# Second layer's expert outputs: summed in PSUM by products with gated selection matrices instead of a round trip through DRAM

## The reference, cut to what matters

```
def moe_ffn(h, ...):                       # per layer; h is the normed, modulated input
    aff = sigmoid(h @ router_w)            # (tokens, 16)
    ... two experts of the best group per token; w = aff of the two / their sum
    gates = one_hot-weighted w             # (tokens, 16)
    for e in range(16):
        he = silu(h @ w_gate[e]) * (h @ w_up[e])      # 1024 -> 512
        y = y + gates[..., e:e + 1] * (he @ w_down[e])  # 512 -> 1024
    return y
# after it: x = x + gate_ffn * y           (gate_ffn: one value per feature, from the conditioning)
# at the end: rms_norm(x, final_norm_g)
```

## Time and profile before

| | us |
|---|---|
| three runs | 3882.34, 1355.3, 1358.66 (median 1358.66) |
| profiled execution, its own time | 1355.8 |
| span of its profile, first to last instruction | 1354.0 |
| PE / weight loads / DVE / ACT / POOL busy | 1126.1 / 529.5 / 428.9 / 297.5 / 64.4 |
| mean granted TensorE clock | 0.921 of 2.4 GHz |
| moved by DMA | 344.03 MB, mean 254 GB/s |

### The profile page before, as it was taken

One profiled execution on the slowest core, in us unless ns is written; L12 is line 12 of the kernel. 1 busy time (PEld: TensorE's weight loads), 2 busy tenths in 40 slices (PEclk: granted clock), 3 DMA queues, 4 the chain that ended last, 5 costly groups with the idle time before them and its releaser, 6 DMA issues.

```text
span 1354.0 us, 15872 instructions
## 1 busy us (share of the span) xinstructions
PE 1126.1 (83%) x6028; PEld 529.5 (39%) x6028; DVE 428.9 (32%) x1021; ACT 297.5 (22%) x694; POOL 64.4 (5%) x71
## 2 busy tenths in 40 slices
PE   4899979978997799999983699988898699994454
PEld 2364433444543333333331446533367233332223
DVE  4111344668714401111110521346673311110003
ACT  2220112426603211111110512013262111110002
POOL 2000011100000200000001000011000100000001
PEclk9899989989999799999986799989899899996676
DMA  9713102939993699999999211306715699999972
GB/s 338 268 63 117 70 0 77 419 126 354 343 378 124 249 337 363 394 396 395 404 392 392 101 62 63 123 2 275 283 36 211 230 374 386 401 415 415 403 289 94
DMA packets 86997, 344.03 MB, mean 254 GB/s; under 512 B 6918, under 2 KB 42187, under 8 KB 64395
## 3 DMA queue, kind: packets, MB, share of 16 engines
q1 hardware_dynamic: 67728, 309.68, 59.2%
q10 hardware_dynamic: 15195, 19.86, 4.3%
q0 software_dynamic: 4000, 13.49, 2.8%
HBM read 300.92 MB, written 42.07 MB: 253 GB/s over the span
## 4 chain that ended last, share of the span: by engine, by line
PE 66%; DMA 18%; DVE 8%; ACT 4%; issue 2%; SPq 1%; POOL 1%; ACTq 1%; POOLq 0%; DVEq 0%
PE ps L946 14%; PE ps L541 12%; DMA ring<-in_exp_w_up 10%; PE ps L969 7%; PE ps L836 6%; PE ps L550 6%; PE ps L484 4%; PE ps L506 3%; DMA slots<-arena 2%; DMA ring<-in_w_mod 2%; PE ps L713 2%; PE ps L729 2%; PE ps L800 1%; PE ps L778 1%; DMA arena<-slots,slot_ids 1%
## 5 line engine op out<-in xcount | busy, mean ns | idle before, releaser
L946 PE MATMUL ps<-ring,arena 128*32 128x256 f32 (+1 forms) x1344 | 197.0, 529 | 47.2 <-DMA ring<-in_exp_w_up 47.2
L541 PE MATMUL ps<-u,ring 128*128 128x512 f32 (+1 forms) x416 | 167.0, 562 | 9.5 <-ACT u L1771 4.0
L484 PE MATMUL ps<-cst,arena 128*128 128x128 f32 (+1 forms) x534 | 99.5, 306 | 64.4 <-DVE arena L1471 33.0
L946 PEld LDWEIGHTS ps<-ring,arena 128*32 128x32 f32 (+1 forms) x1344 | 70.8, 135 | 156.1 <-issue 147.2
L1627 DVE TENSOR_TENSOR arena<-arena,ps 128x128 f32<-128x128 f32 (+1 forms) x59 | 27.2, 503 | 327.0 <-ACT arena L1954 327.0
L484 PEld LDWEIGHTS ps<-cst,arena 128*128 128x128 f32 (+1 forms) x534 | 62.3, 151 | 150.6 <-issue 79.5
L541 PEld LDWEIGHTS ps<-u,ring 128*128 128x128 f32 x416 | 79.8, 193 | 94.2 <-issue 89.3
L969 PE MATMUL ps<-arena 128*32 128x256 f32 (+1 forms) x672 | 94.4, 485 | 1.6 <-ACT arena L1963 1.6
L946 PE MATMUL ps<-arena 128*64 128x512 f32 (+1 forms) x544 | 81.7, 523 | 15.9 <-DMA arena<-in_exp_w_up 15.9
L1954 ACT ACTIVATE arena<-ps 128x256 f32<-128x256 f32 (+1 forms) x44 | 15.3, 348 | 328.1 <-PE ps L946 307.4
L836 PE MATMUL ps<-u,ring 128*128 128x512 f32 (+1 forms) x256 | 83.6, 487 | 1.3 <-DVE h L1452 1.3
(11 more groups left out here) (294 smaller groups left out, 1095.3 us busy)
## 6 DMA issues: line engine op xcount, KB each, us to landing
ring<-in_w_mod SPq DMA_DIRECT2D x24, 2048.0 KB, 10.0
ring<-in_exp_w_gate SPq DMA_DIRECT2D x22, 2048.0 KB, 17.8
ring<-in_exp_w_up SPq DMA_DIRECT2D x22, 2048.0 KB, 21.5
arena<-in_exp_w_down SPq DMA_DIRECT2D x22, 2048.0 KB, 18.2
slots<-zeros SPq DMA_DIRECT2D x4, 6144.0 KB, 42.2
arena<-in_exp_w_gate SPq DMA_DIRECT2D x10, 2048.0 KB, 18.7
u<-in_exp_w_down SPq DMA_DIRECT2D x10, 2048.0 KB, 19.3
arena<-in_exp_w_up SPq DMA_DIRECT2D x10, 2048.0 KB, 24.1
```

The costliest lines, as they stand in the source:

```text
L484: return nc.tensor.transpose(dst, src, ident[0:n, 0:n])
L541: last = nc.tensor.matmul(bank[row:row + width, 0:T - c0], w[:, k, n:n + width], u[:, k, c0:T], start=(k == 0), stop=(k == KT - 1))
L946: last = nc.tensor.matmul(ps[n * part:n * part + n, 2 + b % 2, 0:2 * width].rearrange("p (s n) -> p s n", s=2), x_k, pair[:, :, a:a + widt ...
```

## The change

In the second layer the expert outputs no longer go to DRAM. For each block a selection matrix `sel` (block slots on partitions, 256 tokens on the free axis) is built, which holds the token's gate where the token's slot is this one and zero elsewhere. A product of `sel` with the block's output adds it, in token rows, to four PSUM banks (3, 7 for tile 2; 4, 5 for tile 3) that hold the sum over all blocks.

- `seed_sums`: 8 float32 products for each token tile with the identity put the residual `h` into these banks as the first term.
- `spread_ffn_gates`: 16 products put the feature gates in rows, in the two layouts of a block; ACT copies them. `take_y` then multiplies by them instead of copying.
- `router` on DVE builds diagonal matrices of slots and gates (8 instructions); `spread_rows` on PE makes rows of them on all partitions (2 products); ACT keeps them (`keep_rows`).
- `select` on DVE: two instructions for each block. `combine` on PE: 4 products for a block of 64, 8 for one of 32.
- With four banks taken, blocks no longer alternate between two banks for gate_up and down results.
- The last norm works on token rows: ACT squares with a running sum, DVE scales by root and by the final gain, which two broadcast DMAs bring.
- Gone in the second layer: all `store_y`, the waits for them, the four gathers, `add_experts`, `split_norm("final")` and the transposes back.

```
 def experts(l):   # PE, before the blocks
+    if l == 1: pe.wait_ge(S("ffn_kept"), 2)
...
+def seed_sums(t):
+    for half in range(2):
+        for m in range(4):
+            nc.tensor.matmul(ps[:, sum_bank(t, half), P * m:P * m + P], h[:, 4 * half + m, P * t:P * t + P],
+                             ident, start=(m == 0), stop=False, skip_group_check=True)
+def spread_ffn_gates():
+    pe.wait_ge(S("ut_taken"), ut_count(1, TT - 1, 1) + 1)
+    for n, bank in ((64, 2), (32, 6)):
+        for part in range(P // n):
+            for m in range(n // 16):
+                k = n // 16 * part + m
+                last = nc.tensor.matmul(ps[n * part:n * part + n, bank, P * m:P * m + P],
+                                        mod[:, 1, V_GATE_FFN + k, 1:2].to_broadcast([P, n]), ident,
+                                        start=True, stop=True, tile_position=(0, n * part))
+    last.then_inc(S("ffn_spread"), 1)
...
+def spread_rows():
+    pe.wait_ge(S("diag_ready"), 1)
+    ...
+    nc.tensor.matmul(ps[:, 6, :], ones[:, :], diag[:, 0:2, :], start=True, stop=True)
+    nc.tensor.matmul(ps[:, 0, :], ones[:, :], diag[:, 2:4, :], start=True, stop=True).then_inc(S("rows_spread"), 1)
+def combine(b):
+    n = blocks[b][3]
+    pe.wait_ge(S("sel_ready"), ...); pe.wait_ge(S("y_ready", l), p * nb + (b + 3))
+    order_of = [(2, 0), (3, 1), (3, 0), (2, 1)] if n == 64 else (
+        [(2, 0), (2, 2), (3, 1), (3, 3), (2, 1), (2, 3), (3, 0), (3, 2)])
+    pe.wait_ge(S("combined"), p * (2 * nb) + (2 * b + 4))
+    for i, (t, part) in enumerate(order_of):
+        if 2 * i == len(order_of):
+            last.then_inc(S("combined"), 1)
+            if n == 32: pe.wait_ge(S("combined"), p * (2 * nb) + (2 * b + 5))
+        rows = slice(n * part, n * part + n)
+        width = 8 * n
+        half, at_col = divmod(width * part, 512)
+        last = nc.tensor.matmul(ps[:, sum_bank(t, half), at_col:at_col + width],
+                                sel[rows, b % 2, P * (t - 2):P * (t - 2) + P], y_sb[rows, b % 2, 0:width],
+                                start=False, stop=True, skip_group_check=True)
+    last.then_inc(S("combined"), 1)
...
     gate_up(0)
+    if l == 1: spread_rows()
     turn_hidden(0)
     for b in range(nb - 1):
         gate_up(b + 1)
         if b + 2 < nb:
             turn_x(b + 2)
         project_down(b)
+        if l == 1 and b: combine(b - 1)
         turn_hidden(b + 1)
     project_down(nb - 1)
+    if l == 1:
+        combine(nb - 2)
+        combine(nb - 1)
...
     # PE, order around the experts of a layer
     route(l, range(4, KT))
+    if l == 1: seed_sums(2)
     router(l)
     to_rows(l)
+    if l == 1:
+        seed_sums(3)
+        spread_ffn_gates()
     places(l)
     experts(l)
-    add_experts(l)
-    ... the transposes of the output
+    if l == 0: add_experts(l)
...
     # DVE
     def take_y(b):
         dve.wait_ge(S("down_done", l), p * nb + (nb + b + 1))
-        dve.wait_ge(S(f"y_stored{b % 2}", l), ...)
-        v.tensor_copy(y_sb[:, b % 2, 0:n], ps[:, 6 + b % 2, 0:n]).then_inc(S("y_ready", l), 1)
+        # l == 1:
+        dve.wait_ge(S("combined"), p * (2 * nb) + (2 * b + 2))
+        tt(y_sb[:, b % 2, 0:n], ps[:, down_bank(l, b), 0:n], ffn_rows[blocks[b][3]], ALU.mult) ...
+    def select(b):
+        ...
+        stt(sel_two, slot_rows, slot_at[:, b:b + 1], gate_rows, ALU.is_equal, ALU.mult) ...
+        tt(sel[:, b % 2, :], sel_two[:, 0, :], sel_two[:, 1, :], ALU.add) ...
     hidden(0)
     for b in range(nb - 1):
+        if l == 1: select(b)
         hidden(b + 1)
         take_y(b)
+    if l == 1: select(nb - 1)
     take_y(nb - 1)
...
+    for i, t in enumerate((2, 3)):   # the end on DVE, after two small additions
+        dve.wait_ge(S("root_ready"), i + 1)
         for half in range(2):
-            emptied(v.tensor_copy(tok[...], claim(f"out{t}{half}")))
+            stt(tok[:, t, 512 * half:512 * half + 512], ps[:, sum_bank(t, half), :], small[:, 32 + i:33 + i],
+                final_rows[half], ALU.mult, ALU.mult).then_inc(S("out_ready"), 1)
...
     # ACT, before the blocks of the second layer
+    for half in range(2):
+        act.dma_start(final_rows[half], final_norm_g[...].partition_broadcast(P)) ...
+    act.wait_ge(S("ffn_spread"), 1)
+    nc.scalar.copy(ffn_rows[64], ps[:, 2, :]).then_inc(S("ffn_kept"), 1)
+    nc.scalar.copy(ffn_rows[32], ps[:, 6, 0:256]).then_inc(S("ffn_kept"), 1)
...
-            store_y(b)
+            if l == 0: store_y(b)
...
+    # ACT, after the blocks of the second layer
+    exp_and_ln()
+    act.wait_ge(S("combined"), n_more * (2 * nb) + (2 * nb + 4))
+    for i, t in enumerate((2, 3)):
+        for half in range(2):
+            last = a(x_blk[:, 2 * i + half, :], ps[:, sum_bank(t, half), :], ACT.Square, accum_out=small[...])
+        last.then_inc(S("sums_squared"), 1)
+    for i in range(2):
+        act.wait_ge(S("squares_added"), i + 1)
+        rsqrt(small[:, 32 + i:33 + i], small[:, 32 + i:33 + i], S("root_ready"), 1.0 / DM, small[:, 20:21])
```

More of the change, by code:

```diff
@@ L104, in shape_constants @@
     c[:, C_TOK:C_TOK + TT] = P * np.arange(TT)[None, :] + i[:, None]
+    blocks = expert_blocks(1)
+    assert len(blocks) <= C_CAP - C_SLOT
+    for b, (_, r, a, n) in enumerate(blocks):
+        c[:, C_SLOT + b] = first_row(r) + a + i % n
+        c[:, C_CAP + b] = capacity(1, r)
     return c
@@ L978, in experts @@
                     gate_up(0)
+                    if l == 1:
+                        spread_rows()
                     turn_hidden(0)
@@ L1058, in _ @@
                 route(l, range(4, KT))
+                if l == 1:
+                    seed_sums(2)
                 router(l)
                 to_rows(l)
+                if l == 1:
+                    seed_sums(3)
+                    spread_ffn_gates()
                 places(l)
                 experts(l)
-                add_experts(l)
[L1064 to L1071, removed]
+                if l == 0:
+                    add_experts(l)
         @block.vector
@@ L1696, in _ @@
                 experts(l)
-                add_experts(l, "1mix" if l == 0 else "final")
-            for t in (2, 3):
+                if l == 0:
+                    add_experts(l, "1mix")
+            for i, t in enumerate((2, 3)):
+                dve.wait_ge(S("sums_squared"), i + 2)
+                tt(small[:, 32 + i:33 + i], small[:, 24 + 2 * i:25 + 2 * i], small[:, 25 + 2 * i:26 + 2 * i],
+                   ALU.add).then_inc(S("squares_added"), 1)
+            dve.wait_ge(S("const_landed"), 16 * (3 + n_vec_dmas))
+            for i, t in enumerate((2, 3)):
+                dve.wait_ge(S("root_ready"), i + 1)
                 for half in range(2):
-                    emptied(v.tensor_copy(tok[:, t, 512 * half:512 * half + 512], claim(f"out{t}{half}")))
+                    stt(tok[:, t, 512 * half:512 * half + 512], ps[:, sum_bank(t, half), :], small[:, 32 + i:33 + i],
+                        final_rows[half], ALU.mult, ALU.mult).then_inc(S("out_ready"), 1)
         @block.scalar
@@ L1976, in experts @@
                     silu(0)
+                    if l == 1:
+                        keep_rows()
                     copy_hidden(0)
@@ L2033, in _ @@
                 experts(l)
-            split_norm("final", "y1")
         @block.gpsimd
```

145 lines of the change are left out of this document (121 added, 24 removed).

## The result

The changed kernel took 1338.12 us (median of 4 runs, 1335.06 to 1339.24) against 1356.98 for the kernel before, a ratio of 0.9854 with a 95% interval of 0.9837 to 0.9871: 1.5% faster, which is less than 2% but clear of 1. (The ratio is estimated from the single executions and need not be the quotient of the two medians.) Forecast were 1337 us. The profiled span is 1335.6 us, to the tenth what the sum gave, and that is partly luck: the front cost 1.7 us less than forecast, and an offset of 1.8 us that was in no term cancelled it.

What follows compares the result with a forecast made beforehand. PE was taken to bound the stretch of large blocks and the weight DMAs that of small ones. 1354.0 + 0.9 + 4.7 - 24 = 1335.6 us of span, plus 1.8 around it, gave 1337; range 1323 to 1352.

Steps and rivals of the forecast that it cites:

- Step 1: From the last gate_up to the end of the span, 47.1 us before: 23.7 us saved, taken as 24.
- Step 2: Large blocks: combines on PE release o8's down weights 9.2 us later, queues run dry, last weights land 0.9 us later.
- Step 3: Ahead of the blocks: seeds and gate spread on PE delay the counting product and everything after by 4.7 us.
- DMA alone: Block stretch: queues hold work through the large blocks, the stores' 11.2 us come off in full, 1325.3 us; chance 0.17.
- Products in series: Combines: products of one combine don't overlap, +16.2 us by the last weights, 1360.3 us in all; chance 0.10.
- A second pass: Hidden round trip kept by the change, as a second pass or a wait for x rows; chance about 0.02.
- Steps at nothing: Around the blocks: spread_rows, keep_rows, select, diagonals and single gate_up and down banks cost nothing; spread_rows uncovered would cost 1.93 us.

Runs made afterwards that it cites:

- mixed order: The changed kernel with the second layer's experts reordered so that large and small blocks alternate: 1329.7 us, ratio 0.9793 to the kernel before.
- the one in series: The changed kernel with the four products of each 64-slot combine run one after another, a wait between the two pairs: 1352.0 us, ratio 0.997 to the kernel before.

## Why the prediction was right, step by step

- **Step 1, the end: right.** 23.7 to 24 us were forecast and 24.2 measured (22.9 and 24.5 by the other two profiles; they differ in how long the last gate_up takes, 6.59 and 4.95 us, against 5.24). A 32-slot combine takes 1.45 instead of 1.26 us: its halves last 0.8 each, so the wait between them costs 0.37 and not 0.2. Squares took 2.4 instead of 2.9 us, which makes up for it; the row from which I had their price, L1889, is an exponential with a sum, 0.69 us for 512 columns where a square is 0.60.
- **Step 2, the large blocks: right in both halves.** +9.4 for the issue of down(o8) against 9.2; 113.3 us from there to the last gate_up, forecast 1307.8 - 1194.5 = 113.3. The runs without products, with the stores back and with the mixed order show that it went that way for the reason given. They also show a limit of that reason. The length of the block stretch times its DMA share, divided by the 1.01 of full queues, tells how long the queues were busy, to within 2 us: 216 to 219 us in every kernel without the stores, the changed one and the one in series (0.93 of 238.1) included, and 223 to 226 with them. What comes on top is time in which the queues were dry, some 7 us in the changed kernel and 19 in the one in series. So in the kernel before the DMAs had no slack even in the large blocks, and only the added products gave PE the say there. The Trainium skill, TensorEngine Tiling (Array Packing), Key Properties, states that changing the tiling mode drains the engine. A second drain of 0.2 us per combine, the prediction's estimate, would have made a 64-slot combine 2.1 us; the trace shows 1.92, the products and the usual 0.2 per group.
- **Step 3, the front: direction right, size off, and the match is chance.** 4.7 us forecast; 3.0 measured. Of these only 2.0 are the delay that the sum was about, up to DVE taking up the counting product (1056.84). The terms that were mis-sized are the products: seeds and spread took 4.65 us together where the sum had 6.9. The sixteen spread products took 2.17 us, 0.136 each, where I had 0.215: in column tiles of 64 and 32 they went faster than the full products of the first seeds, 0.25 each at the same granted clock of 1.00. The eight seeds took 2.5 us where I had 3.4, for the clock rose while they ran (windows of the changed kernel):

```profile
1052.00:1054.00 2.00, 2.00 (x14) 2.00 (x14) 1.69 (x11) 1.87 (x2) 0.00 (x0) 0.71 0.30 95
1054.00:1056.00 2.00, 2.00 (x26) 1.71 (x28) 0.72 (x5) 0.00 (x0) 0.00 (x0) 1.00 0.54 175
```

  A good third of the difference is made up by the scatter's extra microsecond, which I had not foreseen. The offset from earlier stages (+1.8, which is in no term) fills the gap to 4.7.
- **The rivals.** DMA alone: its mechanism is refuted for the changed kernel by the dry queue at 1185 to 1205 us and by the stores put back. Its price was mis-sized as well. I took 11.2 us from the share of 16 engines that the second queue showed in the earlier trace rows; the runs give 6.0 (223.3 to 217.3, without products) and 6.8 (to 216.5, before without stores). Had it come true, the time would have been 1328 to 1330 (the prediction's sum with 6.8 for 11.2 gives 1329.7, the run without products 1328.4), and not 1325. One argument that I had against it does not hold: 382 GB/s against 413 is no sign of thin queues, for without products the queues carried 335 to 357 GB/s between 1090 and 1130 us at a DMA share of 1.00 to 1.03. Products in series: 1352.0 measured for the 64-slot blocks alone. The sum with the 32-slot ones was not run. A second pass did not occur.
- **Steps at nothing** held. DVE's busy time in the first stretch rose from 11.8 to 21.1 us with no wait of PE behind it, and spread_rows went into the wait before turn_x(b2), of which 1.44 us were left.

What stays open is the scatter's extra microsecond, and what sets the level of 350 to 390 GB/s in the first 80 us of the blocks. It is there with and without stores, while the later level is 400 to 420.

## What to carry to other kernels

Where one stretch is set by PE and the next by the DMAs, bytes removed from the first are worth only what the queues can use before PE lets go of the buffers. Take the release of a buffer as the clock of such a loop, and count every instruction ahead of it. After a change that loads one engine more, look at the order of work again: an order that was worth nothing before (ratio 0.9999) gave 7 to 9 us after. And end a kernel on what is already in PSUM in the layout of the output: the whole gain here comes from there, 24 us of gathering, turning and norm, of which the front, the block stretch and the offset took back some 6.

## What the runs showed of the hardware

- **Stores beside loads cost less than their share says.** 3.8 MB of result stores (7.47 - 3.67 in the views below) lengthened a stretch of 216.5 us, full of weight loads, by 6.8 us, that is 0.56 MB/us, where the weights by their share of the engines go at 0.40 (the run took away the waits for these stores as well). With the stores put back into the changed kernel, the 1.8 MB of b9 to b18 cost 3.0 to 3.8 us, 0.5 to 0.6 MB/us. The DMA views of the block stretch, first of the kernel before (1084 to 1307 us), then of it without stores (1085 to 1301 us), show the second queue's share of 16 engines at 9.9% and 5.5%. 4.4% of 223 us would be 9.8 us.

```profile
q1 hardware_dynamic: 7230, 81.77, 91.2%
q10 hardware_dynamic: 6233, 7.47, 9.9%
```

```profile
q1 hardware_dynamic: 7215, 81.70, 95.4%
q10 hardware_dynamic: 3136, 3.67, 5.5%
```

- **Four different kernels met one floor.** Without products, mixed order, mixed without products, and the old kernel without stores took 217.3, 216.9 to 217.6, 216.4 and 216.5 us for the same weights.
- **Row tiles overlapped with accumulation into open banks** just as with fresh ones (two products of 64 rows by 256 columns in 0.63 us): four products of 64 rows by 512 columns in 1.92 us, and in 3.95 when kept apart.
